# A feed-forward with two plain tile pairs instead of three, and part of its sums on GpSimd

## The chip, the cores and the metric

The kernel runs on one core of one Trainium2 chip. The metric is the device time of one execution in microseconds (us), from the first to the last instruction and a little around it. A core has five engines with a queue each: TensorE (PE) multiplies, VectorE (DVE), ScalarE (ACT) and GpSimd (POOL) work on elements, SyncE (SP) starts transfers. Each engine takes its instructions strictly in the order in which they were written, and waits where a semaphore has not reached a value.

## What is computed

Two layers, each with two feed-forwards around a mixer. One feed-forward, which the change touches:

```python
def swiglu(x, w_gate, w_up, w_down):
    return (jax.nn.silu(x @ w_gate) * (x @ w_up)) @ w_down
...
h = layer_norm(a * h + 0.5 * swiglu(h, ffn1_w_gate[l], ffn1_w_up[l], ffn1_w_down[l]), ln1_g[l], ln1_b[l])
```

There are 528 tokens (512 and 16 learned ones), the model is 1024 wide, the hidden layer 2816, everything in float32. The last feed-forward runs on 512 tokens.

## The kernel before

**Tiles.** Activations lie transposed: 8 blocks of 128 features by 528 tokens. A hidden tile m is 128 of the 2816 columns, 22 tiles in a feed-forward, and needs one gate piece and one up piece of weights (128 x 1024 numbers each). To keep float32 accuracy each operand is split in a high part (rounded by ScalarE, `w_hi`, `x_hi`) and a low part (what is left, `w_lo`, `x_lo`), and each product is three matmuls: high by high, high by low, low by high.

**Plain and fast pairs.** The first three hidden tiles (`CLASSIC = 3`) are computed plainly, gate and up: 8 blocks x 3 matmuls x 2 halves of the tokens x 2 pieces = 96 matmuls of 264 columns. All others come in pairs of pieces that use a Strassen-Winograd scheme on 2 x 2 blocks (`fast_pair`): seven products p1, p5, p6, p2, p7, p3, p4 in that order instead of eight, of 4 blocks x 3 matmuls each, so 84 matmuls of 264 columns. The price is sums on VectorE. Per feed-forward there are four sums of token blocks, `v_sum` 1 to 4, 128 x 1056 numbers each (v1 = b11 - b12, v3 = b22 - b12, v2 = -v3 - b11, v4 = -v2 - b21), and per pair four sums of weights, `s_sum` 1 to 4, 128 x 512 each (s1 = u_low + u_high, s3 = g_low + u_low, s2 = s1 + g_low, s4 = s2 + g_high). Each is split like everything else: ScalarE copies it to `s_hi` or `v_hi`, VectorE subtracts to `s_lo` or `v_lo`. Three parts of the down projection are fast pairs of 3 blocks (63 matmuls, sums of 128 x 384), the last one is plain.

**What a pair waits for.** Within pair i, p1 needs the low part of the gate piece (`gate_low`), p5 needs s1 and v1 split, p6 needs s2 and v2 split and ScalarE's copy `p1_copied`, p2 the gate's high half, which a GpSimd-issued adding DMA completes, p7 needs s3, v3 and ScalarE's `u2_copied`, p3 needs s4 and `p5_copied`, p4 needs v4, the up piece and VectorE's addition `c22_done`, which itself needs p7. VectorE adds again after p3 (`c12_done`). `banks_free` makes pair 0 wait for the silu and the product of an earlier plain tile.

**Order on the engines.** It is written out by hand. At the start of a feed-forward TensorE runs three pieces block by block (`chunk_products`) while the layer norm before is still finishing the x blocks, then the fourth piece alone (`product`), then the third plain tile (line 758 ff.), then the fast pairs. VectorE and ScalarE do in the meantime what their `ffn` lists (lines 1704 and 1223). In VectorE's loop over the pairs, pair i has the weight sums of pair i+1, the product of the tile before, `gate_low` and s_lo of pair i+1, then `c22`, more low parts, `c12`, s_lo 3 and 4; with `BEHIND` the place of s_lo 2 in that order is chosen.

## Time and profile before

| | before |
|---|---|
| median of 3 runs | 1784.02 us (1783.56 to 1785.22) |
| the profiled execution's span | 1782.4 us |
| TensorE matmul busy | 1770.1 us, 99%, 14462 matmuls |
| VectorE busy | 1434.4 us, 80% |
| ScalarE busy | 1168.0 us, 66% |
| GpSimd busy | 340.0 us, 19% |
| chain that ended last | PE 99% |

The median lies 1.6 us above the span. The profile gives for every instruction its start from the span's start and its duration, and in brackets how long its engine stood idle before it and what ended that. Matmuls overlap: each is shown with some 0.28 us, but they start 0.12 us apart, so lengths on TensorE are read from starts. The four feed-forwards lie at 5 to 332, 545 to 872, 895 to 1222 and 1432 to 1749 us; the last one is that on 512 tokens.

### The profile page before, as it was taken

The numbers are of one execution on the slowest core, as the hardware profiler recorded it, in microseconds if no ns is written. First come the engines' busy times: TensorE is split into PE (matmuls) and PEld (weight loads), VectorE is DVE, ScalarE is ACT, GpSimd is POOL, SyncE is SP. The second block draws the span as 40 slices with busy tenths as digits, with TensorE's granted clock in tenths as the row PEclk, the third lists the DMA queues.
The fourth block names the chain that finished last, engine by engine and source line by source line (L and its number), as shares of the span: only waits on it lengthen the run. The fifth ranks groups of instructions, "written<-read, shape, count | busy, mean of one in ns | idle before, by whom it ended". The sixth has DMA issues, their size and how long they took to land.

```text
span 1782.4 us, 37725 instructions
## 1 busy us (share of the span) xinstructions
PE 1770.1 (99%) x14462; PEld 1733.0 (97%) x14462; DVE 1434.4 (80%) x2577; ACT 1168.0 (66%) x2047; POOL 340.0 (19%) x376
## 2 busy tenths in 40 slices
PE   9999999999999999999999999999999999999997
PEld 9999999999999999999999999999998889999996
DVE  7988888668568988888689888886785689888886
ACT  6767666574357667676576767665743577777764
POOL 2111212311011121111311111113110111111113
PEclk9999999999999999999999999999999999999999
DMA  7675766556565766766556757565665656767662
GB/s 217 141 183 129 177 141 144 150 137 141 115 138 110 170 167 148 169 138 159 145 138 145 176 129 180 134 155 139 141 142 117 147 126 149 185 133 185 133 166 72
DMA packets 112561, 263.54 MB, mean 148 GB/s; under 512 B 10752, under 2 KB 35328, under 8 KB 112384
## 3 DMA queue, kind: packets, MB, share of 16 engines
q1 hardware_dynamic: 66592, 167.86, 32.0%
q0 software_dynamic: 45504, 92.29, 30.8%
q8 instruction: 116, 1.90, 0.4%
q10 hardware_dynamic: 288, 0.98, 0.2%
q14 instruction: 61, 0.50, 0.1%
HBM read 259.00 MB, written 2.10 MB: 146 GB/s over the span
## 4 chain that ended last, share of the span: by engine, by line
PE 99%; DVE 0%; DMA 0%; ACT 0%; issue 0%; ACTq 0%; DVEq 0%
PE PS L680 21%; PE PS L682 21%; PE PS L681 21%; PE PS L655 5%; PE PS L656 4%; PE PS L657 4%; PE PS L609 3%; PE PS L611 3%; PE PS L610 3%; PE PS L619 2%; PE PS L645 2%; PE PS L620 2%; PE PS L987 2%; PE PS L808 1%; PE PS L875 0%; PE PS L902 0%
## 5 line engine op out<-in xcount | busy, mean ns | idle before, releaser
L536 POOL DMA_DIRECT2D w_lo<-in_stream x316 | 269.4, 853 | 1336.8 <-ACT w_lo L1202 1301.9
L1198 ACT ACTIVATE s_hi<-s_sum 128x512 fp32r<-128x512 f32 (+1 forms) x496 | 291.1, 588 | 154.2 <-PE PS L682 145.4
L1701 DVE TENSOR_TENSOR s_lo<-s_sum,s_hi 128x512 fp32r<-128x512 f32 (+1 forms) x496 | 294.4, 633 | 2.9 <-ACT s_hi L1198 2.6
L680 PE MATMUL PS<-v_hi,s_hi 128*128 128x264 f32 (+1 forms) x912 | 258.8, 284 | 0.0
L682 PE MATMUL PS<-v_hi,s_lo 128*128 128x264 f32 (+1 forms) x912 | 258.1, 283 | 0.0
L681 PE MATMUL PS<-v_lo,s_hi 128*128 128x264 f32 (+1 forms) x912 | 258.0, 283 | 0.0
L682 PE MATMUL PS<-x_hi,w_lo 128*128 128x264 f32 (+1 forms) x656 | 185.8, 283 | 0.0
L680 PE MATMUL PS<-x_hi,w_hi 128*128 128x264 f32 (+1 forms) x656 | 185.7, 283 | 0.0
L681 PE MATMUL PS<-x_lo,w_hi 128*128 128x264 f32 (+1 forms) x656 | 185.6, 283 | 0.0
L681 PEld LDWEIGHTS PS<-v_lo,s_hi 128*128 128x128 f32 x912 | 172.2, 189 | 0.0
L680 PEld LDWEIGHTS PS<-v_hi,s_hi 128*128 128x128 f32 x912 | 171.8, 188 | 0.0
L682 PEld LDWEIGHTS PS<-v_hi,s_lo 128*128 128x128 f32 x912 | 171.4, 188 | 0.0
L1208 ACT ACTIVATE w_hi<-raw 128x1024 fp32r<-128x1024 f32 (+2 forms) x152 | 147.1, 968 | 8.0 <-DMA raw<-in_stream 8.0
L1202 ACT ACTIVATE w_lo<-raw 128x512 fp32r<-128x512 f32 (+2 forms) x196 | 143.1, 730 | 0.0
L655 PE MATMUL PS<-x_hi,w_hi 128*128 128x264 f32 (+1 forms) x472 | 140.9, 299 | 0.1
L656 PE MATMUL PS<-x_lo,w_hi 128*128 128x264 f32 (+1 forms) x472 | 139.0, 295 | 0.0
L657 PE MATMUL PS<-x_hi,w_lo 128*128 128x264 f32 (+1 forms) x472 | 138.8, 294 | 0.0
L1263 ACT ACTIVATE PS<-PS 128x264 f32<-128x264 f32 (+1 forms) x124 | 46.3, 373 | 136.4 <-PE PS L682 136.4
L682 PE MATMUL PS<-x_hi,s_lo 128*128 128x264 f32 (+1 forms) x448 | 127.9, 286 | 0.0
L681 PE MATMUL PS<-x_lo,s_hi 128*128 128x264 f32 (+1 forms) x448 | 127.2, 284 | 0.0
L680 PE MATMUL PS<-x_hi,s_hi 128*128 128x264 f32 (+1 forms) x448 | 127.1, 284 | 0.0
L680 PEld LDWEIGHTS PS<-x_hi,w_hi 128*128 128x128 f32 x656 | 123.5, 188 | 0.0
(295 smaller groups left out, 5719.8 us busy)
## 6 DMA issues: line engine op xcount, KB each, us to landing
raw<-in_stream SPq DMA_DIRECT2D x164, 512.0 KB, 4.4
w_lo<-in_stream POOLq DMA_DIRECT2D x160, 256.0 KB, 4.6
spare<-in_stream SPq DMA_DIRECT2D x72, 512.0 KB, 6.8
w_lo<-in_stream POOLq DMA_DIRECT2D x60, 512.0 KB, 7.7
raw<-in_stream SPq DMA_DIRECT2D x48, 384.0 KB, 4.2
spare<-in_stream SPq DMA_DIRECT2D x48, 384.0 KB, 5.3
w_lo<-in_stream POOLq DMA_DIRECT2D x96, 192.0 KB, 4.8
X<-in_x_t SPq DMA_DIRECT2D x8, 264.0 KB, 5.8
```

The source lines that it names most:

```text
L536: pool.dma_start(w_lo[:, slot, to], stream[n // RAWS, n % RAWS, :, part], accum_op=ALU.add).then_inc(lo_added[slot], 16)
L609: nc.tensor.matmul(o, hi, rhs_hi[:, k, tok], start=first, stop=False)
L655: yield nc.tensor.matmul(o, hi, rhs_hi[:, k, tok], start=k == 0, stop=False)
L656: yield nc.tensor.matmul(o, hi, rhs_lo[:, k, tok], start=False, stop=False)
L657: yield nc.tensor.matmul(o, lo, rhs_hi[:, k, tok], start=False, stop=k == n - 1)
L680: nc.tensor.matmul(o, hi[:, w], r_hi, start=start and k == 0, stop=False, skip_group_check=True)
L681: nc.tensor.matmul(o, hi[:, w], r_lo, start=False, stop=False, skip_group_check=True)
L682: m = nc.tensor.matmul(o, lo[:, w], r_hi, start=False, stop=stop and k == last, skip_group_check=True)
L1198: nc.scalar.activation(s_hi[:, j - 1, w], s_sum[:, j - 1, w], ACT.Copy).then_inc(S["s_hi_done"], 1)
L1202: nc.scalar.activation(w_lo[:, n % SLOTS, to], of, ACT.Copy, scale=-1.0).then_inc(S["raw_neg"], 1)
L1208: nc.scalar.activation(w_hi[:, n % SLOTS, to], of, ACT.Copy).then_inc(S["raw_hi"], 1)
L1701: V.tensor_tensor(s_lo[:, j - 1, w], s_sum[:, j - 1, w], s_hi[:, j - 1, w].bitcast(F32), ALU.subtract).then_inc(S["s_lo_done"], 1)
```

## The change

`CLASSIC` goes from 3 to 2: the third hidden tile of each feed-forward becomes a fast pair, which makes 32 of them instead of 31. The token sums lose their own buffer. They now lie where the hidden tiles and their sums are stored later (`v_sum_a`, `v_sum_b`), and the sums of the first hidden tiles (`t_sums(1)`) are done after them. v1 and v4 are formed by GpSimd (`v_pool`), v3 and v2 by VectorE, v2 now with the other sign, which its split turns back. s3 of every pair is formed by GpSimd (`sum_three`), between its two adding DMAs of the pair. ScalarE and VectorE get a new order at the start of a feed-forward (VectorE's is the last piece of the diff). SP's loads wait for s3 as well.

```diff
-CLASSIC = 3
+CLASSIC = 2
-BEHIND = 2
+BEHIND = 3
...
+            def v_pool(l, f):
+                span = OWN if l == DEPTH - 1 and f == 1 else ALL
+                at = 2 * (2 * l + f)
+                b11, b12, b21, _ = x_blocks(span)
+                wait_x_full(pool, l, f)
+                nc.gpsimd.tensor_tensor(v_sum(1, span), b11, b12, ALU.subtract).then_inc(S["v_pool_done"], 1)
+                pool.wait_ge(S["v_sum_done"], at + 2)
+                nc.gpsimd.tensor_tensor(v_sum(4, span), v_sum(2, span), b21, ALU.subtract).then_inc(S["v_pool_done"], 1)
+
+            def sum_three(l, f, i):
+                i_all, gate = fast_index(l, f, i), fast_piece(l, f, i)
+                if i_all > 0:
+                    pool.wait_ge(S["s_lo_done"], 4 * (i_all - 1) + 3)
+                wait_raw(pool, gate)
+                wait_raw(pool, gate + 1)
+                nc.gpsimd.tensor_tensor(s_sum[:, 2, low_half(gate)], raw_halves(gate)[0], raw_halves(gate + 1)[0],
+                                        ALU.add).then_inc(S["s3_done"], 1)
...
                 product(3, 3, x_hi, x_lo, KC, span=span).then_inc(S["piece_done"], 1)
-                m = CLASSIC - 1
-                for j in range(2):
-                    n = FP + 2 * m + j
-                    wait_low(pe, n)
-                    pe.wait_ge(S["prod_done" if j else "silu_done"], F22 + m - 1)
...
                 for i in range(FAST):
                     banks_free(l, f, i)
                     fast_pair(l, f, i, span)
...
-                v_sums(l, f, span, (3, 1))
+                v_sums(l, f, span)
+                w_sums(l, f, 0, (1, 2))
                 classic_product(0)
-                gate_low(FP + 4)
-                h_low(l, f, 0, span)
-                v_sums(l, f, span, (2, 4))
...
+                v_low(l, f, span, 1)
+                sum_low(l, f, 0, 1)
+                gate_low(first)
+                w_sums(l, f, 0, (4,))
+                v_low(l, f, span, 2)
+                sum_low(l, f, 0, 2)
...
+                classic_product(1)
+                w_sums(l, f, 1, (1,))
+                gate_low(fast_piece(l, f, 1))
+                add_p5(0)
```

The rows below are instructions in the order of each engine, with what they wait for; `v_hi<-v_sum_a` is the rounding of v1 or v2, `v_hi<-v_sum_b` that of v3 or v4, `silu<-PS` the first plain tile. ScalarE at the start of the second feed-forward (the layer norm's last tile in the first row), before:

```order
L1404 ACTIVATE X<-xhat,par 128x528
L1160 ACT_TABLE_LOAD
L1160 ACTIVATE silu<-PS 128x528 [waits piece_done]
L1208 ACTIVATE w_hi<-raw 128x1024 [waits raw_full0,piece_done]
L1202 ACTIVATE w_lo<-raw 128x512
L1190 ACTIVATE v_hi<-v_sum 128x1056 [waits v_sum_done] x2
L1172 ACTIVATE h_hi<-prod 128x264 [waits prod_done]
L1208 ACTIVATE w_hi<-raw 128x1024 [waits raw_full1,piece_done]
L1202 ACTIVATE w_lo<-raw 128x512
L1160 ACTIVATE silu<-PS 128x528 [waits piece_done]
```

and now:

```order
L1440 ACTIVATE X<-xhat,par 128x528
L1226 ACTIVATE v_hi<-v_sum_a 128x1056 [waits v_pool_done]
L1226 ACTIVATE v_hi<-v_sum_b 128x1056 [waits v_sum_done]
L1195 ACT_TABLE_LOAD
L1195 ACTIVATE silu<-PS 128x528 [waits piece_done]
L1248 ACTIVATE w_hi<-raw 128x1024 [waits raw_full0,piece_done]
L1242 ACTIVATE w_lo<-raw 128x512
L1238 ACTIVATE s_hi<-s_sum 128x512 [waits p5_acc,s_sum_done]
L1226 ACTIVATE v_hi<-v_sum_a 128x1056 [waits v_sum_done]
L1248 ACTIVATE w_hi<-raw 128x512 [waits raw_full1,piece_done]
L1242 ACTIVATE w_lo<-raw 128x512
L1238 ACTIVATE s_hi<-s_sum 128x512 [waits p6_acc,s_sum_done]
```

The two roundings of token sums have come ahead of the table load and the silu, and the first of them waits for GpSimd. VectorE at the same place, before:

```order
L1652 TENSOR_TENSOR v_sum<-X 128x1056 [waits early_full,x_full_done]
L1654 TENSOR_TENSOR v_sum<-X 128x1056
L1565 SCALAR_TENSOR_TENSOR prod<-PS,silu 128x528 [waits piece_done,silu_done]
L1695 TENSOR_TENSOR w_lo<-raw,w_hi 128x512 [waits raw_hi]
L1596 TENSOR_TENSOR h_lo<-prod,h_hi 128x264 [waits h_hi_done]
L1657 SCALAR_TENSOR_TENSOR v_sum<-v_sum,X 128x1056 [waits v_sum_done,early_full,x_full_done]
L1660 SCALAR_TENSOR_TENSOR v_sum<-v_sum,X 128x1056 [waits v_sum_done]
L1695 TENSOR_TENSOR w_lo<-raw,w_hi 128x512 [waits raw_hi]
L1666 TENSOR_TENSOR v_lo<-v_sum,v_hi 128x1056 [waits v_hi_done] x2
L1565 SCALAR_TENSOR_TENSOR h_raw<-PS,silu 128x528 [waits h_lo_done,piece_done,silu_done]
```

and now:

```order
L1679 TENSOR_TENSOR v_sum_b<-X 128x1056 [waits early_full,x_full_done]
L1681 TENSOR_TENSOR v_sum_a<-v_sum_b,X 128x1056 [waits v_sum_done]
L1704 TENSOR_TENSOR s_sum<-raw 128x512 [waits raw_full1,s_lo_done]
L1708 TENSOR_TENSOR s_sum<-s_sum,raw 128x512 [waits s_sum_done,raw_full0,s_lo_done]
L1601 SCALAR_TENSOR_TENSOR prod<-PS,silu 128x528 [waits piece_done,silu_done]
L1691 TENSOR_TENSOR v_lo<-v_sum_a,v_hi 128x1056 [waits v_hi_done]
L1724 TENSOR_TENSOR s_lo<-s_sum,s_hi 128x512 [waits s_hi_done]
L1718 TENSOR_TENSOR w_lo<-raw,w_hi 128x512 [waits raw_hi]
L1711 TENSOR_TENSOR s_sum<-s_sum,raw 128x512 [waits s_sum_done,s_lo_done]
L1688 SCALAR_TENSOR_TENSOR v_lo<-v_sum_a,v_hi 128x1056 [waits v_hi_done]
```

Two weight sums stand ahead of the first product, and the low part of pair 0's gate (`w_lo<-raw,w_hi`) behind the low parts of v1 and s1. GpSimd at the same place, now (before, these are eight DMAs without arithmetic):

```order
L558 DMA w_lo<-in_stream 128x1024 [waits raw_neg]
L613 TENSOR_TENSOR v_sum_a<-X 128x1056 [waits early_full,x_full_done]
L615 TENSOR_TENSOR v_sum_b<-v_sum_a,X 128x1056 [waits v_sum_done]
L558 DMA w_lo<-in_stream 128x512 [waits raw_neg]
L624 TENSOR_TENSOR s_sum<-raw 128x512 [waits raw_full1,raw_full0,s_lo_done]
L558 DMA w_lo<-in_stream 128x512 [waits raw_neg] x2
L624 TENSOR_TENSOR s_sum<-raw,spare 128x512 [waits raw_full3,raw_full1,s_lo_done]
L558 DMA w_lo<-in_stream 128x512 [waits raw_neg] x2
```

The two token sums precede pair 0's first DMA, and each pair's s3 stands between its two.

## Rows read from the trace of the kernel before

**Rows 1.** Page, busy time, share of the span, instructions of each engine.

```profile
PE 1770.1 (99%) x14462; PEld 1733.0 (97%) x14462; DVE 1434.4 (80%) x2577; ACT 1168.0 (66%) x2047; POOL 340.0 (19%) x376
```

**Rows 2.** Timeline, TensorE: start us, duration us; plain tiles, and pairs' first matmuls.

```profile
569.22 0.28 PE L609 MATMUL PS<-x_hi,w_hi 128*128 128x264 f32 x1
...
580.82 0.28 PE L680 MATMUL PS<-x_hi,w_hi 128*128 128x264 f32 x1
...
591.02 0.28 PE L680 MATMUL PS<-x_hi,w_hi 128*128 128x264 f32 x1
...
1455.06 0.40 PE L609 MATMUL PS<-x_hi,w_hi 128*128 128x512 f32 x1
...
1466.18 0.28 PE L680 MATMUL PS<-x_hi,w_hi 128*128 128x256 f32 x1
...
1556.75 0.28 PE L680 MATMUL PS<-x_hi,w_hi 128*128 128x256 f32 x1
...
1566.70 0.28 PE L680 MATMUL PS<-x_hi,w_hi 128*128 128x256 f32 x1
```

**Rows 3.** Groups by form, GpSimd's arithmetic: count, busy us, mean ns.

```profile
L543 POOL TENSOR_TENSOR w_lo<-raw,w_hi 128x1024 fp32r<-128x1024 f32 x16 | 39.5, 2474 | 34.8 <-ACT w_hi L1208 34.8
L582 POOL TENSOR_TENSOR X<-X,mean 128x528 f32<-128x528 f32 x8 | 10.3, 1300 | 22.4 <-ACT mean L1365 22.4
L599 POOL TENSOR_TENSOR X<-X,mean 128x512 f32<-128x512 f32 x4 | 4.9, 1264 | 19.6 <-ACT mean L1365 19.6
```

**Rows 4.** Timeline around 327 us, GpSimd.

```profile
327.04 5.23 POOL L543 TENSOR_TENSOR w_lo<-raw,w_hi 128x1024 fp32r<-128x1024 f32 x2 [2.68 <-ACT w_hi L1208]
```

**Rows 5.** Timeline of the same stretch, VectorE.

```profile
327.84 2.17 DVE L1596 TENSOR_TENSOR h_lo<-h_raw,h_hi 128x528 fp32r<-128x528 f32 x1 [0.71 <-ACT h_hi L1172]
...
329.93 2.49 DVE L1780 TENSOR_TENSOR w_rank<-par,w_rank 128x128 fp32r<-128x128 f32 x1
```

**Rows 6.** Timeline around 544 us, GpSimd, then VectorE.

```profile
543.87 2.58 POOL L582 TENSOR_TENSOR X<-X,mean 128x528 f32<-128x528 f32 x2 [5.54 <-ACT mean L1365]
...
544.53 1.10 DVE L1871 SCALAR_TENSOR_TENSOR X<-xhat,par,PS 128x264 f32<-128x264 f32 x2 [0.35 <-PE PS L824]
```

**Rows 7.** Timeline, ScalarE, start of the second feed-forward.

```profile
558.73 0.81 ACT L1404 ACTIVATE X<-xhat,par 128x528 f32<-128x528 f32 x1
559.56 1.28 ACT L1160 ACT_TABLE_LOAD   x1
563.13 0.61 ACT L1160 ACTIVATE silu<-PS 128x528 f32<-128x528 f32 x1 [2.29 <-PE PS L645]
563.64 1.06 ACT L1208 ACTIVATE w_hi<-raw 128x1024 fp32r<-128x1024 f32 x1
...
565.11 2.05 ACT L1190 ACTIVATE v_hi<-v_sum 128x1056 fp32r<-128x1056 f32 x2
```

**Rows 8.** Timeline, VectorE, the same place.

```profile
559.64 0.71 DVE L1933 TENSOR_TENSOR x_lo<-X,x_hi 128x528 fp32r<-128x528 f32 x1 [1.33 <-ACT X L1404]
560.27 1.25 DVE L1652 TENSOR_TENSOR v_sum<-X 128x1056 f32<-128x1056 f32 x1
561.44 1.25 DVE L1654 TENSOR_TENSOR v_sum<-X 128x1056 f32<-128x1056 f32 x1
```

**Rows 9.** Timeline, VectorE, sums for the third pair of that feed-forward.

```profile
592.93 0.69 DVE L1679 TENSOR_TENSOR s_sum<-spare 128x512 f32<-128x512 f32 x1
593.53 0.69 DVE L1682 TENSOR_TENSOR s_sum<-raw,spare 128x512 f32<-128x512 f32 x1
594.13 0.69 DVE L1685 TENSOR_TENSOR s_sum<-s_sum,raw 128x512 f32<-128x512 f32 x1
594.92 0.69 DVE L1688 TENSOR_TENSOR s_sum<-s_sum,raw 128x512 f32<-128x512 f32 x1
595.53 0.70 DVE L1565 SCALAR_TENSOR_TENSOR h_raw<-PS,silu 128x528 f32<-128x528 f32 x1
...
598.98 0.43 DVE L1753 TENSOR_TENSOR PS<-PS,p_copy 128x264 f32<-128x264 f32 x1
```

**Rows 10.** Timeline, last feed-forward's second pair: VectorE's c22, then TensorE.

```profile
1484.95 0.43 DVE L1753 TENSOR_TENSOR PS<-PS,p_copy 128x256 f32<-128x256 f32 x1
...
1485.48 0.35 PE L680 MATMUL PS<-v_hi,w_hi 128*128 128x256 f32 x1 [0.41 <-issue]
```

**Rows 11.** Timeline, VectorE's c22 in the second feed-forward's third pair.

```profile
608.65 0.44 DVE L1753 TENSOR_TENSOR PS<-PS,p_copy 128x264 f32<-128x264 f32 x1 [0.30 <-PE PS L682]
```

**Rows 12.** Page, DMA issues: KB each, us to landing.

```profile
raw<-in_stream SPq DMA_DIRECT2D x164, 512.0 KB, 4.4
w_lo<-in_stream POOLq DMA_DIRECT2D x160, 256.0 KB, 4.6
```

**Rows 13.** Busy time by stretch: PE, PEld, DVE, ACT, POOL, granted clock, DMA.

```profile
1773.00:1777.00 4.00, 0.00 (x0) 0.00 (x0) 3.95 (x7) 3.40 (x5) 3.65 (x3) 1.00 0.48 181
1777.00:1782.00 5.00, 0.00 (x0) 0.00 (x0) 1.88 (x3) 2.57 (x4) 0.00 (x0) 0.55 0.73 275
569.20:580.80 11.60, 11.60 (x98) 11.60 (x97) 11.33 (x17) 9.25 (x14) 2.56 (x3) 1.00 0.74 159
580.80:590.90 10.10, 10.10 (x85) 10.10 (x84) 9.96 (x18) 6.81 (x13) 1.70 (x2) 1.00 0.89 251
590.90:601.10 10.20, 10.20 (x87) 10.20 (x86) 10.03 (x19) 7.91 (x15) 1.70 (x2) 1.00 0.63 122
```

**Rows 14.** Timeline, TensorE, first matmuls of the program.

```profile
5.50 0.42 PE L620 MATMUL PS<-x_hi,w_lo 128*128 128x264 f32 x1
5.71 0.42 PE L619 MATMUL PS<-x_hi,w_hi 128*128 128x264 f32 x1
```

More of the change, by code:

```diff
@@ L163, in kind_of @@
     if r < 2 * CLASSIC or r >= LAST_DOWN:
-        return "first" if n < SLOTS else "added" if r < SLOTS else "half" if r < 2 * CLASSIC else "split"
+        return "first" if n < SLOTS else "added" if r < SLOTS else "split"
     return "up" if r % 2 else "gate"
@@ L207, in dma_adds @@
 def dma_adds(n):
-    return kind_of(n) in ("added", "half", "gate", "up")
+    return kind_of(n) in ("added", "gate", "up")
 def engine_splits(n):
-    return kind_of(n) in ("split", "half", "gate")
+    return kind_of(n) in ("split", "gate")
 def added_value(n):
@@ L430, in norm_bias, with v_sum, x_blocks @@
             return par[:, c:c + 1]
+        def v_sum(j, span):
+            return (v_sum_a if j < 3 else v_sum_b)[:, (j - 1) % 2, :, 0:halved(span)[1]]
+        def x_blocks(span):
+            early, late = tokens(span, 0), tokens(span, 1)
+            return X[:, 0:BAND, early], X[:, 0:BAND, late], X[:, BAND:KC, early], X[:, BAND:KC, late]
         def t_block(main, x, k, span):
@@ L485, in raw_halves, with wait_x_full @@
             return [raw[:, buffer_of(n), low_half(n)], raw[:, buffer_of(n), high_half(n)]]
+        def wait_x_full(eng, l, f):
+            if l == 0 and f == 0:
+                for k in range(KC):
+                    eng.wait_ge(x_loaded[k], 16)
+            else:
+                eng.wait_ge(S["x_full_done"], (l * LN_PER + 2 * f) * (KC - EARLY))
+                eng.wait_ge(S["early_full"], (l * LN_PER + 2 * f) * EARLY)
         def wait_stream(eng, l, idx):
@@ L591, in _ @@
                     pad(n // LAYER_PIECES)
+                if kind_of(n) == "gate" and place_of(n)[2] == 0:
+                    v_pool(*place_of(n)[:2])
                 if dma_adds(n):
@@ L595, in _ @@
                     split(n)
+                if kind_of(n) == "gate":
+                    sum_three(*place_of(n))
             pool.wait_ge(S["mean_first_copied"], DEPTH * LN_PER)
@@ L1665, in v_low @@
                 dve.wait_ge(S["v_hi_done"], 4 * (2 * l + f) + V_ORDER.index(j) + 1)
-                V.tensor_tensor(v_lo[:, j - 1, :, 0:n], v_sum[:, j - 1, :, 0:n], v_hi[:, j - 1, :, 0:n].bitcast(F32),
-                                ALU.subtract).then_inc(S["v_lo_done"], 1)
+                high = v_hi[:, j - 1, :, 0:n].bitcast(F32)
+                if j == 2:
+                    x = V.scalar_tensor_tensor(out=v_lo[:, 1, :, 0:n], in0=v_sum(2, span), scalar=-1.0, in1=high,
+                                               op0=ALU.mult, op1=ALU.subtract)
+                else:
+                    x = V.tensor_tensor(v_lo[:, j - 1, :, 0:n], v_sum(j, span), high, ALU.subtract)
+                x.then_inc(S["v_lo_done"], 1)
             def w_sums(l, f, i, js=S_ORDER):
@@ L1743, in ffn @@
                         add_down(l, f, i - 1, span)
-                    elif was == "up":
-                        fast_prod(l, f, was_a, 2 - ps, span)
+                    else:
+                        fast_prod(l, f, was_a, bank_set(i - 1), span)
                     if follows:
@@ L1763, in ffn @@
                         h_low(l, f, sum(PHASES[was_a]), span)
-                    dve.wait_ge(S["p3_acc"], i_all + 1)
-                    dve.wait_ge(S["u2_copied"], i_all + 1)
-                    V.tensor_tensor(PS[ps][:, 1, 0:n], PS[ps][:, 1, 0:n], u2_copy[:, 0:n],
-                                    ALU.add).then_inc(S["c12_done"], 1)
-                    if i == 0:
-                        t_low(l, f, 1, span)
-                    elif was == "up" and kind == "up":
+                    add_u2(i)
+                    if i == 2:
+                        t_low(l, f, CLASSIC - 1, span)
+                    if was == "up" and kind == "up":
                         t_low(l, f, was_a, span)
```

183 lines of the change are left out of this document (84 added, 99 removed).

## The prediction

> **What bounds the kernel now.** I read the busy shares first: TensorE 99%, VectorE 80% [rows 1]. The chain of waits consists of matmuls, so any matmul taken away shortens the run, unless TensorE comes to wait. It never did so for more than a fraction of a microsecond between the first and the last matmul. The one wait of that kind is the place to look at [rows 10]: in the last feed-forward's second pair, VectorE's addition c22 began at 1484.95, took 0.43, and product p4, which needs it, stood 0.41 us. So VectorE is the next limit already, at the start of a feed-forward. The busy time by stretch says the same: VectorE is busy 11.33 of 11.60, 9.96 of 10.10 and 10.03 of 10.20 us in the stretches of the third plain tile and of the first two pairs [rows 13]. Where it had caught up, in the third pair, it waited only 0.30 us for TensorE before c22 [rows 11]. p4 comes one product (12 x 0.121 = 1.45 us) after p7, so that pair had some 1.2 us of slack.
>
> **What goes on TensorE.** Lengths come from starts. Third plain tile: 580.82 - 569.22 = 11.60 us; a fast pair: 591.02 - 580.82 = 10.20 us [rows 2]. Saved: 1.40 us, three times. In the feed-forward on 512 tokens 1466.18 - 1455.06 = 11.12 against a settled pair's 1566.70 - 1556.75 = 9.95: 1.17 us. Together 5.4 us. If nothing waited, the span would be 1782.4 - 5.4 = 1777.0.
>
> **What GpSimd's additions cost.** VectorE loses s3, 0.60 us a pair by the distance of starts. But s2 needs s1 and s4 needs s2; a sum behind the one it depends on starts 0.79 after it, not 0.60 (594.13 to 594.92) [rows 9]. Three sums in a chain take 0.79 + 0.79 + 0.60 = 2.2 us against 2.6 for four: VectorE saves 0.4. GpSimd needs 1.26 us for 512 numbers and 2.4 for 1024 [rows 3]; the slope gives 2.5 us for a token sum of 1056. These are not hidden beside VectorE. GpSimd's two subtractions began at 327.04, and VectorE's subtraction of 528 numbers, normally 0.7, took 2.17; the next, of 128 numbers, took 2.49 [rows 4, 5]. Each ended just after one of GpSimd's. So a VectorE instruction with both inputs in SBUF stands until GpSimd's ends, and GpSimd got in again between two VectorE instructions. One with an input in PSUM did not stand: 1.10 us for two, while GpSimd worked [rows 6]. An s3 therefore costs VectorE up to 1.2 us less 0.4, and less what falls on the product from PSUM (0.6), so 0.2 to 0.8. In the settled pairs this fits in the slack of 1.2. At the start it doesn't.
>
> **The start of a feed-forward, step by step** (second one; all in us on the old clock). X is complete at 559.54 [rows 7]. VectorE's `x_lo` goes first, at 559.64 [rows 8], then GpSimd's v1 has the port, 560.3 to 562.7. VectorE: v3 to 563.9, v2 to 565.2 (1.25 each), s1 to 565.8. GpSimd's v4, released by v2, gets in: to 568.15. VectorE: s2 to 568.8, the first product to 569.4.
> ScalarE: v1's rounding 562.8 to 563.8, v3's to 565.0 (2.05 for two), table load 1.28 to 566.3, silu to 566.9. Before, the table load lay in idle time at 559.56 and the silu ended at 563.74 [rows 7]. Then the gate's rounding and negative to 568.4 (0.95 and 0.52 apart). That doesn't decide, VectorE is later.
> VectorE: low part of v1 to 570.5; GpSimd's s3 of pair 0 gets in, to 571.7; low part of s1 to 572.3; low part of the gate to 573.0. Only then can pair 0 start. TensorE is free at 569.22: **3.8 us of idle**. Behind it VectorE has s4, then the low parts of v2, s2, v3, s3, v4, s4 (each v 1.25, each s 0.6), which end at 578.9, 0.5 to 1.7 us ahead of their products, ScalarE's copies no earlier than needed (the raw data of pair 1's gate may load only behind s3 and the up piece's negative at 571.7, and land 4.4 us later [rows 12]; the copy for p7 is ready at 578.7, its time). The second product, s1 and `gate_low` of pair 1 with one more s3 of GpSimd in between end at 581.4, c22 at 581.8: p4 0.15 late. Pair 1 starts at 583.3, 3.95 late.
> In pair 1 VectorE now also has h_lo of tile 0 and the four sums of tile 1 (2.0), then pair 2's sums with GpSimd's s3; c22 comes at 593.4 where p4 is due at 592.0, and two ScalarE copies come 0.3 late by then: 1.4 us. Pair 2 just holds. Pair 3 has behind it two t_lo (1.2 each): 0.6 late. From pair 4 on (smaller sums) VectorE has caught up. Sum for this feed-forward: 3.95 + 1.4 + 0.6 = 6.0. The third is alike.
> In the first feed-forward X lies ready from the load, v1 and v3 are done while TensorE runs its chunks, the table is loaded. There pair 0 starts 0.25 late, ends 0.45 late, then 1.4 and 0.6: 2.5. In the last one a token half is 256, so TensorE is 2% quicker and VectorE hardly; X is complete only 8.8 us ahead of pair 0 instead of 9.7, which adds 0.8, and its next pairs had no slack before [rows 10]: 7.
>
> **Sum.** 2.5 + 6 + 6 + 7 = 21.5 of waits, less 5.4: +16. Span 1782.4 + 16 = 1798.4, and 1.6 outside it: **1800 us**. Bounds of the waits: each of the seven or so VectorE steps that GpSimd delays at a start may cost nothing where an instruction reads PSUM, or its whole length; I take +-2 us a feed-forward, 1792 to 1808.
> Costed at nothing: adding DMAs (landing 4.6 us after issue [rows 12], pair 0's gate at 573.9 for 577.3), the moved buffers, SP's new wait (s3 is formed before the sums that release the same load), GpSimd's issue behind s3 in settled pairs, where it stood idle most of the time (busy 19% [rows 1]).
>
> **Rivals.** *Little blocking* (the stalls of rows 5 are peculiar to those instructions, or GpSimd is not served between VectorE's). Then v2 ends at 562.8 and VectorE is in time, but ScalarE's order stays: roundings, table load, silu to 566.2, gate to 567.7, and its list up to p1's copy ends at 573.9, due at 572.1, and the copy for p7 a little later still. 2.1 us each in the middle two, 2.7 in the last, none in the first: +6.9 - 5.4, **1785.5**. For it: all of GpSimd's larger arithmetic before are 28 instructions [rows 3], a thin basis. Against it: both instructions of rows 5 end with GpSimd's. The Trainium skill's page "SBUF — State Buffer" (section "SBUF: two separate sides") says that VectorE and GpSimd share a port pair which one instruction holds for its whole length, and that a VectorE instruction with two SBUF inputs is among those that need it; by that this rival has no room, and the trace agrees at 2.17 us.
> *All hidden.* The order was laid so that the sums come in time, and I misjudge several waits by 4 us. Then 1784.0 - 5.4 = **1778.6**. For it: DVE was busy only 80%. Against: the 0.41 us wait that is there already [rows 10].
> *The clock falls.* A wait of 3.8 us might lower the granted clock. After the last matmul it stayed at 1.00 until 1777 (4.7 us) and was 0.55 in the mean of the 5 us after [rows 13]; at the low level, 1.2 GHz, matmuls start 0.21 apart instead of 0.12 [rows 14], so each microsecond there loses 0.44. With a low stretch as long as the wait, in three feed-forwards: 3 x 3.8 x 0.44 = 5 us on top, **1805**. The Trainium skill's page "TensorE: Matmul & The Clock Gate" (section "HAM oscillation — how this bites in real kernels") says that idle gaps of TensorE halve its clock, so that a wait is paid again in the matmuls after it. This trace has no wait of that length with matmuls behind it; by the page this rival would be the rule, by the end of the trace the exception.
>
> **Chances.** Forecast (6 us a start) 0.66; little blocking 0.12; all hidden 0.10; clock 0.12. The time is the likeliest's, 1800. The range leaves out the all-hidden case and the far end of the clock's: 1784 to 1808. A measurement here can tell 0.2% (3.6 us). Slower: forecast, clock and a bit of the little-blocking case, 0.81; same 0.09 (most of little blocking); faster 0.10.
>
> **What would show it.** In the profile of the changed kernel: GpSimd's `v_sum` rows near 2.5 us right behind the last X tile, and `v_sum`, `s_sum` and `v_lo` rows on VectorE of 2 to 3.6 us beside them instead of 1.25 and 0.7; the table load behind two roundings of v; TensorE idle some 3.8 us ahead of pair 0 in the middle two feed-forwards and more in the last, under 0.5 in the first; 1.4 us ahead of p4 in pair 1 of all four; no matmuls of a third plain tile. Wrong would be: VectorE rows of normal length beside GpSimd's (little blocking), or waits that go on in the settled pairs, which would make it slower than 1808.

## The result and the profile after

| | before | after |
|---|---|---|
| median | 1783.79 us (4 runs beside it) | 1817.26 us (1816.73 to 1817.70, 4 runs) |
| ratio | | 1.0185, 95% interval 1.0171 to 1.0200 |
| span profiled | 1782.4 us | 1815.8 us |

The change makes the kernel 33.5 us slower. The direction was forecast, the size was not: 16 us, with a range that ended at 1808.

The busy shares and the chain, from the page of the changed kernel (beside [rows 1]):

```profile
PE 1780.6 (98%) x14462; PEld 1737.0 (96%) x14462; DVE 1539.7 (85%) x2477; ACT 1179.1 (65%) x2075; POOL 522.0 (29%) x512
...
PE 87%; DVE 7%; issue 3%; ACT 1%; DMA 0%; SPq 0%; DVEq 0%; ACTq 0%
```

VectorE has 100 instructions fewer than before and is busy 105 us longer: its instructions got longer. What TensorE waited for (line waited at, what for, total us, times, longest):

```profile
PE PS L726 <- DVE w_lo L1718: 12.4, 4, 3.9
PE PS L726 <- issue: 6.3, 8, 1.0
PE PS L726 <- DVE PS L1741: 3.2, 13, 0.4
```

The first line is the wait ahead of pair 0 (`gate_low`), which was forecast. The second, for which the view names no releaser, is p4 of pairs 1 and 3 in each of the four feed-forwards: it starts 0.10 us behind the end of VectorE's c22 every time. The third is new: 13 waits for c22 (L1741), all over the settled pairs (pair 4 and later), where nothing had been forecast.

The start of the second feed-forward on VectorE (start, duration, line, operation, output and inputs):

```profile
564.79 3.01 DVE L1969 TENSOR_TENSOR x_lo<-X,x_hi 128x528 fp32r<-128x528 f32 x1 [1.35 <-ACT X L1440]
...
571.00 2.78 DVE L1708 TENSOR_TENSOR s_sum<-s_sum,raw 128x512 f32<-128x512 f32 x1
573.70 0.69 DVE L1601 SCALAR_TENSOR_TENSOR prod<-PS,silu 128x528 f32<-128x528 f32 x1
574.32 2.75 DVE L1691 TENSOR_TENSOR v_lo<-v_sum_a,v_hi 128x1056 fp32r<-128x1056 f32 x1
576.99 0.68 DVE L1724 TENSOR_TENSOR s_lo<-s_sum,s_hi 128x512 fp32r<-128x512 f32 x1
577.59 0.68 DVE L1718 TENSOR_TENSOR w_lo<-raw,w_hi 128x512 fp32r<-128x512 f32 x1
```

GpSimd and ScalarE at the same place:

```profile
564.77 2.46 POOL L613 TENSOR_TENSOR v_sum_a<-X 128x1056 f32<-128x1056 f32 x1 [8.87 <-ACT X L1440]
570.34 2.89 POOL L615 TENSOR_TENSOR v_sum_b<-v_sum_a,X 128x1056 f32<-128x1056 f32 x1 [3.11 <-DVE v_sum_a L1681]
...
574.39 1.55 POOL L624 TENSOR_TENSOR s_sum<-raw 128x512 f32<-128x512 f32 x1
```
```profile
570.11 1.28 ACT L1195 ACT_TABLE_LOAD   x1
```

Each of the three sums on GpSimd has one VectorE instruction beside it that ends 0.6 to 1.1 us, about its own usual length, after GpSimd's end (567.23, 573.23, 575.94): 3.01 us where 0.71 is usual, 2.78 where 0.69 is, 2.75 where 1.25 is. A product with an input in PSUM is not held off. The one above (573.70) does not show it, for it lies between two sums of GpSimd, but this one lies wholly within a sum (GpSimd, then VectorE), and no other product of this size beside GpSimd's operations took more than 0.71 us:

```profile
583.70 1.65 POOL L624 TENSOR_TENSOR s_sum<-raw,spare 128x512 f32<-128x512 f32 x1
```
```profile
584.11 0.69 DVE L1601 SCALAR_TENSOR_TENSOR h_raw<-PS,silu 128x528 f32<-128x528 f32 x1
```

`w_lo` at 577.59 is what pair 0 waits for:

```profile
578.42 0.36 PE L726 MATMUL PS<-x_hi,w_hi 128*128 128x264 f32 x1 [3.77 <-DVE w_lo L1718]
```

And what followed on TensorE, from the table by stretches (stretch, its length, busy time and count of PE, PEld, DVE, ACT and POOL, granted clock, DMA share, GB/s):

```profile
578.99:582.30 3.31, 3.31 (x18) 3.31 (x17) 3.31 (x4) 1.87 (x4) 0.00 (x0) 0.50 1.02 280
937.50:940.70 3.20, 3.20 (x16) 3.20 (x16) 3.20 (x5) 1.84 (x4) 0.00 (x0) 0.50 1.03 267
1483.60:1486.80 3.20, 3.20 (x17) 3.20 (x16) 3.20 (x5) 2.06 (x4) 0.00 (x0) 0.50 1.04 295
```

Behind each of the three waits of nearly 4 us the granted clock was 0.50, which is 1.2 GHz, for 3.4 us. In the first feed-forward, with a wait of under 1 us there, it was not.

**Where the time went.** I read the lengths of all pairs from the starts of their first matmuls, before and after, per feed-forward (us):

| | forecast, sum | 1st | 2nd | 3rd | 4th | sum |
|---|---|---|---|---|---|---|
| plain pair replaced | -5.4 | -1.4 | -1.4 | -1.4 | -1.2 | -5.5 |
| pair 0 starts later | 12.5 | 1.4 | 4.1 | 4.1 | 4.7 | 14.3 |
| pair 0 longer (low clock) | 0.6 | 0.1 | 1.6 | 1.6 | 1.6 | 4.9 |
| pair 1 longer | 5.6 | 1.3 | 0.9 | 0.9 | 1.1 | 4.1 |
| pair 3 longer | 2.4 | 1.1 | 1.1 | 1.1 | 1.2 | 4.6 |
| all later pairs | 0 | 2.7 | 2.6 | 3.0 | 3.0 | 11.3 |
| sum | 16 | 5.1 | 8.9 | 9.2 | 10.5 | 33.7 |

The forecast was short in two places above all: the settled pairs and the clock. The 3.0 us of the last feed-forward are net: its later pairs are 3.9 us longer, and 0.9 us that its first two fast pairs had lost before are taken off. So the later pairs cost 12.3 us in all, of which the down pairs make 7.5.

### The profile page after: what moved, and what is told of

The parts are those of the page before. It is cut to its first block, busy times and chain, and to the rows that moved or that the text cites. A ratio compares the mean times of both kernels' runs of the same rounds, so it can differ in the third digit from the quotient of the medians.

```text
span 1815.8 us, 37981 instructions
## 1 busy us (share of the span) xinstructions
PE 1780.6 (98%) x14462; PEld 1737.0 (96%) x14462; DVE 1539.7 (85%) x2477; ACT 1179.1 (65%) x2075; POOL 522.0 (29%) x512
## 4 chain that ended last, share of the span: by engine, by line
PE 87%; DVE 7%; issue 3%; ACT 1%; DMA 0%; SPq 0%; DVEq 0%; ACTq 0%
PE PS L726 21%; PE PS L727 20%; PE PS L728 20%; PE PS L701 4%; PE PS L702 4%; PE PS L703 4%; PE PS L655 3%; PE PS L657 3%; PE PS L656 3%; DVE s_lo L1724 1%; PE PS L1022 1%; DVE X L1672 1%; DVE v_lo L1691 1%; DVE s_sum L1704 1%; PE PS L843 1%
## 5 line engine op out<-in xcount | busy, mean ns | idle before, releaser
L1724 DVE TENSOR_TENSOR s_lo<-s_sum,s_hi 128x512 fp32r<-128x512 f32 (+1 forms) x512 | 312.6, 647 | 0.4
L726 PE MATMUL PS<-v_hi,s_hi 128*128 128x264 f32 (+1 forms) x960 | 273.6, 285 | 0.0
L727 PE MATMUL PS<-v_lo,s_hi 128*128 128x264 f32 (+1 forms) x960 | 272.4, 284 | 0.0
L728 PE MATMUL PS<-v_hi,s_lo 128*128 128x264 f32 (+1 forms) x960 | 272.3, 284 | 0.0
L727 PE MATMUL PS<-x_lo,w_hi 128*128 128x264 f32 (+1 forms) x688 | 195.6, 284 | 0.0
L624 POOL TENSOR_TENSOR s_sum<-raw,spare 128x512 f32<-128x512 f32 (+1 forms) x124 | 185.8, 1499 | 1.0 <-DMA spare<-in_stream 0.9
L727 PEld LDWEIGHTS PS<-v_lo,s_hi 128*128 128x128 f32 x960 | 182.6, 190 | 0.0
L726 PEld LDWEIGHTS PS<-v_hi,s_hi 128*128 128x128 f32 x960 | 182.1, 190 | 0.2 <-ACT u_copy L1313 0.2
L728 PEld LDWEIGHTS PS<-v_hi,s_lo 128*128 128x128 f32 x960 | 181.5, 189 | 0.0
L1718 DVE TENSOR_TENSOR w_lo<-raw,w_hi 128x512 fp32r<-128x512 f32 (+1 forms) x128 | 153.3, 1197 | 0.0
L702 PE MATMUL PS<-x_lo,w_hi 128*128 128x264 f32 (+1 forms) x472 | 138.9, 294 | 0.0
```

The costliest lines, as they stand in the source:

```text
L624: nc.gpsimd.tensor_tensor(s_sum[:, 2, low_half(gate)], raw_halves(gate)[0], raw_halves(gate + 1)[0], ALU.add).then_inc(S["s3_done"], 1)
L702: yield nc.tensor.matmul(o, hi, rhs_lo[:, k, tok], start=False, stop=False)
L726: nc.tensor.matmul(o, hi[:, w], r_hi, start=start and k == 0, stop=False, skip_group_check=True)
L727: nc.tensor.matmul(o, hi[:, w], r_lo, start=False, stop=False, skip_group_check=True)
L728: m = nc.tensor.matmul(o, lo[:, w], r_hi, start=False, stop=stop and k == last, skip_group_check=True)
L1718: V.tensor_tensor(w_lo[:, n % SLOTS, part], raw_halves(n)[0], w_hi[:, n % SLOTS, part].bitcast(F32), ALU.subtract).then_inc(lo_done[n % SL ...
```

## The experiments

**Undoing the parts.** Three kernels each put a part of GpSimd's work back on VectorE; a fourth puts one part alone into the kernel before. Theory A is that a GpSimd operation shuts VectorE out; theory B that two plain tile pairs simply leave too little time.

*Weight sum back:*

```diff
-                if kind_of(n) == "gate":
-                    sum_three(*place_of(n))
...
+                    elif j == 3:
+                        wait_raw(dve, gate)
+                        wait_raw(dve, gate + 1)
+                        V.tensor_tensor(s[2], g_low, u_low, ALU.add).then_inc(S["s3_done"], 1)
+                        continue
```

> The changed kernel with the third weight sum of every pair back on VectorE (order 1, 3, 2, 4), GpSimd keeping the two token sums. Theory A (a GpSimd sum and a VectorE sum shut each other out, and what VectorE loses is what TensorE waits): the up pairs 8, 10, 14 and 16, which are 0.26 to 0.37 us longer each in the changed kernel, go back to their old length (2.7 us less per feed-forward, 10.8 in all), pairs 1 to 3 lose part of their lateness, the 3.8-us waits ahead of pair 0 stay within 1.5 us since the two token sums are still on GpSimd: 1793 to 1803 us. Theory B (VectorE loses nothing to GpSimd; with two plain tiles there is simply too little TensorE work ahead of pair 0, and in the settled pairs VectorE has no room): VectorE gets one more sum per pair, so the time is that of the changed kernel or above it: 1815 to 1830 us.

Measured: 1794.94 us, ratio to before 1.0059 (1.0044 to 1.0074), 22.3 less than the changed kernel. The settled up pairs are back at 10.17 us, all of them (9.95 in the last feed-forward). The waits of TensorE:

```profile
PE PS L724 <- DVE w_lo L1721: 9.4, 4, 3.0
```

No wait for c22 is left. Theory B, which wanted 1815 or more, is out as the whole cause. The start wait shrank from 3.8 to 2.9 us, and the clock behind it differed (second, third and fourth feed-forward, first the matmul behind the wait, then the stretches):

```profile
572.30 0.56 PE L724 MATMUL PS<-x_hi,w_hi 128*128 128x264 f32 x1 [2.86 <-DVE w_lo L1721]
926.81 0.56 PE L724 MATMUL PS<-x_hi,w_hi 128*128 128x264 f32 x1 [2.86 <-DVE w_lo L1721]
1467.07 0.36 PE L724 MATMUL PS<-x_hi,w_hi 128*128 128x256 f32 x1 [2.95 <-DVE w_lo L1721]
```
```profile
572.30:577.80 5.50, 5.50 (x25) 5.50 (x26) 5.50 (x7) 3.78 (x7) 0.25 (x1) 0.50 0.93 263
...
926.80:929.80 3.00, 2.99 (x13) 3.00 (x14) 3.00 (x4) 1.85 (x4) 0.00 (x0) 0.50 0.82 206
...
1467.10:1473.00 5.90, 5.90 (x49) 5.71 (x49) 5.90 (x8) 4.25 (x9) 0.35 (x1) 1.00 0.92 265
```

After two equal waits of 2.86 us matmuls ran at the low clock for 5.9 us once (to 578.2) and for 3.0 us once (to 929.8); after one of 2.95 us they never did. Pair 0 was 12.92, 11.60 and 10.42 us long.

*Token sums back* (v1 ahead of the other sums, v4 behind the fourth weight sum of pair 0; the weight sum stays on GpSimd):

```diff
-                if kind_of(n) == "gate" and place_of(n)[2] == 0:
-                    v_pool(*place_of(n)[:2])
...
+                V.tensor_tensor(v_sum(1, span), b11, b12, ALU.subtract).then_inc(S["v_pool_done"], 1)
```

> The changed kernel with the first and the fourth token sum on VectorE (the first ahead of the other sums, the fourth behind the fourth weight sum of pair 0) and the third weight sum of each pair still on GpSimd. Theory A (blocking): VectorE's sums and roundings ahead of pair 0 take their old 1.2 us instead of 2.7 to 3.0; of the three 3.8-us waits at most 1.5 us each is left, and the granted clock does not fall behind them (three times 1.55 us more); the settled pairs stay 0.26 us longer: 1798 to 1806 us. Theory B (too little work ahead of pair 0): VectorE now has two sums of 1.25 us more ahead of pair 0, the waits grow from 3.8 to about 5 us and the clock still falls: 1817 to 1824 us.

Measured: 1812.87 us (ratio 1.0162, 1.0147 to 1.0177), only 4.4 less than the changed kernel. Both theories missed. Pair 0 started 2.3 us earlier in the later three feed-forwards, as A wants, but waits came back inside pair 0, which was 12.0 us long in all four:

```profile
PE PS L724 <- ACT PS L1292: 4.7, 4, 1.5
```

The copy of the first product (L1292) now comes too late, because ScalarE's list is late as well. The settled pairs stay long, as theory A says, with 13 waits for c22.

*Both back*, the two edits above together, so that GpSimd does none of these sums and only the missing plain tile pair and the new order are left:

> The changed kernel with all three kinds of sum back on VectorE, so that GpSimd does no arithmetic; still two plain tile pairs per feed-forward. It separates the two halves of the change. Theory A (blocking is all of the loss): what is left is the saving of a plain tile pair per feed-forward, 5.4 us in all, less a short wait for pair 0: 1778 to 1786 us. Theory B (the missing plain tile pair is the loss): pair 0 waits 3 us or more in the middle feed-forwards, and the time stays above 1795 us.

Measured: 1787.76 us, 1.0020 (1.0011 to 1.0029), 1.8 above theory A's range. So of the 33.5 us, the weight sum makes 22.3, the token sums 7.2 with the weight sum gone (4.4 with it there), and the missing plain tile with its new order 3.7, where it was to save 5.4. The saving exists: in the third feed-forward pair 0 starts 23.44 us behind the feed-forward's start where the third plain tile began at 23.44, so that nothing is late, and a pair has taken the place of 11.60 us. It is eaten in pairs 0 and 1:

```profile
PE PS L722 <- ACT PS L1290: 4.4, 3, 1.5
PE PS L722 <- ACT u_copy L1309: 1.3, 2, 0.8
```

*The weight sum alone, in the kernel before* (three plain tile pairs, old order):

```diff
-                    elif j == 3:
-                        wait_raw(dve, gate)
-                        x = V.tensor_tensor(s[2], g_low, u_low, ALU.add)
...
+                if kind_of(n) == "gate":
+                    sum_three(*place_of(n))
```

> The kernel before (three plain tile pairs, all token sums on VectorE) with one edit: the third weight sum of every pair is formed by GpSimd. Theory A (blocking): the up pairs 8, 10, 14 and 16 and some down pairs grow as in the changed kernel, 2.7 us per feed-forward, 10.8 in all, and pairs 1 and 3 by up to 1 us each: 1793 to 1802 us. Theory B (GpSimd's sums lie beside VectorE's without a price): VectorE has one sum less per pair and the time is 1781 to 1785 us.

Measured: 1806.23 us, 1.0128 (1.0111 to 1.0145): 22.1 us for one edit, the same as its removal gave from the other side. A expected 9 to 18. Of the 5.2 us in the second feed-forward 2.6 lie in its settled pairs and 2.5 in pairs 0, 1 and 2. One settled pair of it, GpSimd, then VectorE, then TensorE:

```profile
695.11 1.60 POOL L593 TENSOR_TENSOR s_sum<-raw,spare 128x512 f32<-128x512 f32 x1
```
```profile
694.86 2.15 DVE L1596 TENSOR_TENSOR t_raw<-prod 128x264 f32<-128x264 f32 x1
...
699.55 0.43 DVE L1767 TENSOR_TENSOR PS<-PS,p_copy 128x264 f32<-128x264 f32 x1
```
```profile
699.79 0.28 PE L695 MATMUL PS<-x_hi,s_lo 128*128 128x264 f32 x1
700.09 0.36 PE L693 MATMUL PS<-v_hi,w_hi 128*128 128x264 f32 x1
```

The same instructions of the same pair in the kernel before:

```profile
686.81 0.42 DVE L1580 TENSOR_TENSOR t_raw<-prod 128x264 f32<-128x264 f32 x1
...
690.27 0.44 DVE L1753 TENSOR_TENSOR PS<-PS,p_copy 128x264 f32<-128x264 f32 x1 [0.41 <-PE PS L682]
```
```profile
691.54 0.28 PE L680 MATMUL PS<-v_hi,w_hi 128*128 128x264 f32 x1
```

There VectorE waited 0.41 us for TensorE before c22. With GpSimd's sum an operation of 0.42 us stood 1.7 us longer, c22 came with no pause ahead of it at 699.55, ended at 699.98, and p4 started at 700.09, 0.30 behind the last matmul instead of 0.12. With its second matmul, again 0.07 late, that is the 0.26 us by which this up pair is longer.

The down pairs lose more. The last one ahead of an up pair had no room even before: its c22 followed the operation ahead of it without a pause, and the pair took 7.80 us where 7.65 is usual. GpSimd's sum at 655.36 (1.61 us) makes it 8.11; before, then with that sum:

```profile
650.53 0.44 DVE L1753 TENSOR_TENSOR PS<-PS,p_copy 128x264 f32<-128x264 f32 x1
```
```profile
656.14 1.38 DVE L1709 TENSOR_TENSOR w_lo<-raw,w_hi 128x512 fp32r<-128x512 f32 x1
```

`w_lo` is twice as long as usual, and c22 comes 6.36 us behind the pair's start instead of 6.04. Twelve such pairs make 3.7 of the 7.5 us of the down pairs.

**Blocking or lateness?** A moved sum also arrives later: GpSimd takes 1.6 us for it, VectorE 0.7. To tell the two apart GpSimd forms the sum into a buffer that nobody reads:

```diff
+                nc.gpsimd.tensor_tensor(scrap[:, 0:blocks_of(i) * P], raw_halves(gate)[0], raw_halves(gate + 1)[0],
+                                        ALU.add).then_inc(S["s3_done"], 1)
```

> The kernel before, complete and unchanged on every engine but GpSimd, which in addition forms the third weight sum of every pair once more, into a buffer that nobody reads, released by the same wait as in the kernel with that sum on GpSimd. VectorE still forms its own, so no engine waits for GpSimd's result. Theory A (blocking: the GpSimd sum holds VectorE off for its own length): VectorE has even one sum more to do than in the kernel with the sum moved (1806 us), so the time is 1806 to 1815 us, and single VectorE operations grow from 0.4 to 0.7 us up to 1.6 to 2.2 us beside each GpSimd sum. Theory C (late result: what costs time in the moved sum is that it takes GpSimd 1.6 us instead of 0.7 and that ScalarE and VectorE then wait for it): nobody waits here, 1783 to 1786 us.

Measured: 1820.15 us, 1.0201 (1.0186 to 1.0216). Nobody reads this result, and the kernel before loses 36 us. One engine does wait for it, other than the text above says: SyncE loads a weight buffer anew only behind the sum that reads it, as in the changed kernel. By the trace this is not what costs the time: three of SyncE's waits ended with a sum, 7.5 us together, ScalarE stood 6.6 us for these weight loads (8.0 before) and VectorE 0.2 (0.7 before), and TensorE's waits of over 0.4 us in the fast pairs all lie at p4, which starts 0.10 us (up) or 0.15 us (down) behind the end of VectorE's c22. So lateness is out. The time is 5 us above my upper end; 14 us lie between it and the kernel with the sum moved, where VectorE has one sum fewer. The row of busy shares, and one pair on GpSimd and VectorE:

```profile
PE 1786.2 (98%) x14462; PEld 1737.3 (96%) x14462; DVE 1560.9 (86%) x2577; ACT 1171.3 (64%) x2047; POOL 495.1 (27%) x500
```
```profile
690.24 1.61 POOL L595 TENSOR_TENSOR scrap<-raw,spare 128x512 f32<-128x512 f32 x1
```
```profile
689.92 2.49 DVE L1703 TENSOR_TENSOR s_sum<-s_sum,raw 128x512 f32<-128x512 f32 x1
```

VectorE runs the same 2577 instructions as before [rows 1] and is busy 126.5 us longer: 1.02 us for each of the 124 sums, which themselves last 1.33 (384 numbers) to 1.61 us.

*One input in place of two:*

```diff
+                nc.gpsimd.tensor_copy(scrap[:, 0:blocks_of(i) * P], raw_halves(gate)[0]).then_inc(S["s3_done"], 1)
```

> The kernel before with an unread copy of 512 values per partition by GpSimd in each pair, at the place of the extra sum of the other run: one input in place of two. If any GpSimd read and write holds VectorE off, the copy costs as the sum does, 10 to 30 us in all; if only operations with two inputs do, the time is that of the kernel before, 1783 to 1787 us. I lean to the second, as VectorE's own operations with one input from PSUM are not lengthened in the trace.

Measured: 1789.42 us, 1.0028 (1.0017 to 1.0040), between the ranges of the two cases. I had leaned to the wrong side. A copy, for which SyncE's loads wait as they did for the sum, does hold VectorE off:

```profile
PE 1771.2 (99%) x14462; PEld 1732.7 (97%) x14462; DVE 1475.8 (83%) x2577; ACT 1167.4 (65%) x2047; POOL 414.7 (23%) x500
```
```profile
688.95 0.92 POOL L595 COPY scrap<-raw 128x512 f32<-128x512 f32 x1
```
```profile
688.69 1.48 DVE L1593 TENSOR_TENSOR t_raw<-h_raw,prod 128x264 f32<-128x264 f32 x1
```

0.43 became 1.48. But a copy is over in 0.94 us, VectorE lost 41 us in all (0.33 a copy), and that fits nearly everywhere into its slack: settled pairs stayed at 10.17, and the 5.2 us lie in the first two pairs.

**Can two plain tile pairs pay at all?** From here on all sums are VectorE's. ScalarE first, with its table load in idle time and the first copy ahead of a rounding:

```diff
+                if (l, f) != (0, 0):
+                    nc.scalar.activation(warm[:, 1:2], warm[:, 0:1], ACT.Silu)
                 v_high(l, f, 1, span)
...
                 v_high(l, f, 4, span)
+                act.wait_ge(S["p1_acc"], fast_index(l, f, 0) + 1)
+                nc.scalar.activation(PS[bank_set(0)][:, 0, 0:halved_n], PS[bank_set(0) + 1][:, 0, 0:halved_n],
+                                     ACT.Copy).then_inc(S["p1_copied"], 1)
                 sum_high(l, f, 0, 3)
```

> Two plain tile pairs and all sums on VectorE (the kernel that took 1787.8 us), with two edits on ScalarE: the table for silu is loaded ahead of the first token rounding, where ScalarE is idle for 2.0 us, and the copy of pair 0's first product stands ahead of the third weight rounding and the second silu. There TensorE waited 1.4 to 1.5 us for that copy in three feed-forwards, and up to 0.8 us for the next copy, and pair 1 was 0.5 us long. If ScalarE's queue is what ate the 5.4 us saving, those waits go but for some 0.4 us each that VectorE's roundings still cost: 1779.5 to 1783 us. If VectorE is as late as ScalarE, 1785 to 1788 us.

Measured: 1783.57 us, 0.9997 (0.9987 to 1.0006), 4.2 less than without the two edits (what each gave is not separated), level with before and just above the range given. Pair 0 was still 0.6 to 0.7 us too long in the first three feed-forwards and 1.3 in the last, pair 1 0.5 to 0.8.

```diff
-                w_sums(l, f, 0, (4,))
...
-                V.tensor_tensor(v_sum(4, span), v_sum(2, span), x_blocks(span)[2], ALU.subtract).then_inc(S["v_pool_done"], 1)
                 v_low(l, f, span, 2)
                 sum_low(l, f, 0, 2)
+                w_sums(l, f, 0, (4,))
...
+                V.tensor_tensor(v_sum(4, span), v_sum(2, span), x_blocks(span)[2], ALU.subtract).then_inc(S["v_pool_done"], 1)
```

> As the run with the table and the copy early, and on VectorE the fourth weight sum and the fourth token sum of pair 0 stand behind the second pair of roundings instead of ahead of it, so that TensorE's third product of pair 0 has its operands 1.9 us earlier. If VectorE's order held the rest, the whole saving of a plain tile pair in four feed-forwards is seen: 1778 to 1780.5 us. If not, it is equal to the other within 1 us.

Measured: 1788.46 us, 1.0023 (1.0014 to 1.0033), worse by 5, which neither case had. The move made a wait somewhere else:

```profile
PE PS L722 <- ACT PS L1281: 4.6, 3, 1.6
```

ScalarE's copy of the first product stood behind the rounding of v4, which waited for the sum I had moved back. So ScalarE's list was put right, with VectorE's later order and, in a second kernel, with its old one:

```diff
-                v_high(l, f, 4, span)
...
+                copy_p1(0)
                 sum_high(l, f, 0, 3)
                 act.wait_ge(S["piece_done"], FP + 3)
                 silu_of(2, span)
+                copy_p5(0)
+                v_high(l, f, 4, span)
                 sum_high(l, f, 0, 4)
```

Behind that come the p6 copy and only then pair 1's gate; in pair 1 the copies stand ahead of the roundings too.

> Two plain tile pairs, all sums on VectorE, the silu table early, VectorE's order of the run with the roundings early, and ScalarE's order mended: in that run (1788.5 us) TensorE waited 1.5 us in three feed-forwards for the copy of pair 0's first product, since the copy stood behind the fourth token rounding, which itself waits for the token sum that had been moved back. Now both copies of pair 0 that TensorE waits for stand ahead of that rounding and of the weight roundings of pair 1, and in pair 1 the copies stand ahead of the roundings too. If these orders are all that kept the saving of the plain tile pair (1783.6 us in the best run so far), pairs 0 and 1, which are 0.7 and 0.7 us too long there, return to 10.2 us: 1778 to 1781 us. If VectorE is late for pair 1 whatever the order, 1781 to 1784 us.

> As the run with both orders, but VectorE keeps its old order (fourth weight sum and fourth token sum ahead of the second pair of roundings). TensorE's third product of pair 0 then has its operands 1.9 us later: it waits 0.3 to 0.4 us there per feed-forward, 1.5 us in all, more than with both orders: 1780 to 1783 us. If VectorE's order doesn't matter, equal within 0.5 us.

Measured: 1784.60 us (1.0003, 0.9994 to 1.0012) and 1783.71 us (0.9998, 0.9989 to 1.0007). Neither differs from before, nor clearly from the other, and each lies 0.6 to 0.7 us above the range given for it. In the first, the two pieces I was after did go: pair 0 is 10.2 us in the first feed-forward and 10.5 in the others, with no wait for a copy. The time went to pair 1, 11.3 us long, at one instruction (TensorE, then VectorE):

```profile
589.42 0.36 PE L722 MATMUL PS<-v_hi,w_hi 128*128 128x264 f32 x1 [0.91 <-issue]
```
```profile
588.88 0.44 DVE L1762 TENSOR_TENSOR PS<-PS,p_copy 128x264 f32<-128x264 f32 x1
```

p4 waits for c22, as in the kernel before [rows 10], and c22 stood in a queue that had not paused since the token sums. So I moved c22 ahead in pair 1, and then in pairs 2 and 3 too:

```diff
+                    if i == 1:
+                        add_p5(1)
                     if was == "down":
                         add_down(l, f, i - 1, span)
                     else:
                         fast_prod(l, f, was_a, bank_set(i - 1), span)
+                    if i in (2, 3):
+                        add_p5(i)
...
-                    add_p5(i)
+                    if i not in (1, 2, 3):
+                        add_p5(i)
```

> As the run with both orders (1784.6 us), with one more move on VectorE: in pair 1 the sum that adds the copied fifth product in PSUM, which TensorE's last product of the pair waits for, stands behind the four weight sums of pair 2 instead of behind three further operations. In that run TensorE waited 1.2 us per feed-forward there, with the sum at 588.88 us and its input ready since 586.8 us. If the wait only sat in the order, it goes, 4 x 1.1 us: 1779 to 1781 us, faster than the kernel before by 0.2%. If VectorE, busy without a pause since the token sums, is late as a whole, the wait moves into pair 2 or 3 and the time stays at 1783 to 1785 us.

> As the run before it (1782.5 us), with the same sum in PSUM moved ahead in pairs 2 and 3 as well: there it now stands directly behind the product and the hidden sums of the tile before, ahead of the weight rounding. In the profile of that run the wait had moved from pair 1 (1.2 us) to pair 2 (0.5 us) and pair 3 (0.27 us), 3.1 us over four feed-forwards; VectorE runs without a pause from the token sums to pair 3. If VectorE has caught up by pair 4, those waits go: 1779.5 to 1781 us, 0.2% faster than the kernel before. If it is still behind, they move on to pairs 4 and 5: 1782 to 1783 us.

Measured: 1782.51 us (0.9992, 0.9983 to 1.0001) with pair 1 alone, 1780.23 us (0.9979, 0.9970 to 0.9988; 1779.60 to 1781.80 in 11 runs) with all three. The first step moved the wait on, as its second case said, to 0.5 us in pair 2 and 0.27 in pair 3, though the time fell by 2.1 us, to between the two cases; the second step ended it, but for 0.2 us in pair 3 (0.5 in the last feed-forward). The last kernel is faster than the kernel before by 4.1 us, and than the changed one by 37. What TensorE still waits for in its fast products:

```profile
PE PS L722 <- issue: 1.1, 1, 1.1
PE PS L722 <- DVE w_lo L1739: 0.3, 1, 0.3
PE PS L722 <- ACT u_copy L1323: 0.2, 1, 0.2
```

The wait of 1.1 us is p4 of pair 0 in the last feed-forward, again 0.10 us behind the end of c22. Whether the new orders would speed up the kernel with three plain tile pairs as well was not run. Its trace leaves little for them: its first two fast pairs lose 0.9 us in the last feed-forward and next to nothing in the others.

## Why the prediction was wrong, point by point

- **TensorE's saving, 5.4 us: right.** 1.43 us in each of the long feed-forwards (11.60 less 10.17). Losses elsewhere hid it: the last experiment is 4.1 us faster than before, with pairs 0 and 3 still 3.2 us too long over the four feed-forwards.
- **How GpSimd and VectorE meet: right.** VectorE stands for the length of a GpSimd sum if it has both inputs in SBUF, not if it reads PSUM, and the run with the unread sum shows that this holding off, not the late result, costs the time. The page "SBUF — State Buffer" of the Trainium skill (section "SBUF: two separate sides") says that one instruction holds the ports that the two engines share for its whole length; the forecast cited it against the little-blocking rival, and it was borne out at 2.15 us where 0.42 is usual.
- **The wait of 3.8 us ahead of pair 0: right**, 3.77 in the second feed-forward. Not all of its working was: I had VectorE's `x_lo` go before GpSimd's v1. They were released together, GpSimd started at 564.77, and `x_lo` took 3.01 us. VectorE's v3 and v2 then met nothing, so the sum came out alike; that this error cost nothing was luck. GpSimd's token sums took 2.46 to 2.9 us for the 2.5 that I had put ([rows 3] have 2.47 us for 1024 numbers, not 2.4).
- **The first feed-forward, 0.25 us late: too small.** It was 1.4. Some of this is scatter: the same distance is 23.4 to 24.2 us in the seven kernels with two plain pairs and no GpSimd sums, 25.2 here, 23.8 before. At least 1 us is left: I took the work done while TensorE runs its chunks as free. With the token sums back on VectorE and only the weight sum on GpSimd it is 23.4 us, so the loss comes from GpSimd's token sums.
- **Pair 1, 1.4 us, and pair 3, 0.6 us:** 4.1 instead of 5.6 and 4.6 instead of 2.4 over the four.
- **The settled pairs, 0: this step failed, by 11.3 us.** I set the cost of an s3 at 0.2 to 0.8 us against 1.2 us of slack. In the up pair shown the slack was about right: VectorE waited 0.41 us, and c22 ended at 690.71, 0.73 us earlier than p4 needed it (691.54, less the 0.10 that passes from the end of c22 to p4 in the waits). Together 1.1 us. The cost was not right. I had taken 1.26 us for GpSimd's sum from operations that ran mostly undisturbed [rows 3]; here the mean for 512 numbers was 1.60 (why it is longer no run shows). And I had subtracted a share for a product from PSUM that falls beside it. In four up pairs of a feed-forward (10, 12, 20 and 22 of the changed kernel) it doesn't: GpSimd's sum starts behind its adding DMA, at 695.11 in the pair shown, after the product and among the sums of the hidden tile. There VectorE stands for the whole 1.7 us, 2.15 - 0.42. Of that the missing fourth sum gives back 0.3: c22 comes 8.37 us behind the pair's start instead of 7.46, and its 0.41 us of pause are gone. 1.3 us against 1.1: with the slower start of p4 behind it a loss of 0.26 in each of these pairs. And the slack was not the same everywhere: I had read it in one up pair [rows 11], and the down pair ahead of an up pair had none. One figure for all pairs hid both.
- **The clock: a rival with 0.12, and it happened.** 1.6 us each in three feed-forwards, 4.8 together; I had priced it at 5. The page "TensorE: Matmul & The Clock Gate" of the Trainium skill (section "HAM oscillation — how this bites in real kernels") says that a wait of TensorE can be followed by matmuls at half its clock; by it this rival was the rule, by the end of the trace [rows 13] the exception. The page was right for this kernel; the end of the trace, where the clock held for 4.7 us, was a bad witness. It is no certainty either: of the waits between matmuls in these runs, the three of the changed kernel (3.77, 3.77, 3.93 us), one of 2.37 in the second experiment (1.6 us behind its end) and two of 2.86 in the first were followed by the low clock, one of 2.95 and all of up to 1.6 us were not.
- **The range.** Even with every bound of mine at its end it stopped at 1808, for the settled pairs had no term with an upper bound. "Waits that go on in the settled pairs, which would make it slower than 1808" was written down as what would prove me wrong, and had no chance in the sum.
- **What was costed at nothing for the loads: right.** SyncE waited nine times for an s3, 95.5 us together, but ScalarE stood only 2.8 us for these weight loads, less than before (8.0).
